# A three-layer transformer step in fp32: convolution jobs fed by the centered residual with both norms' rows applied behind PSUM, and a ring of nine weight slots for the experts

## The reference, cut to what matters

```python
# end of layer b
h = layer_norm(ALPHA * h + gate * y, ln_g[1], ln_b[1])        # eps 1e-5
# start of layer c
h1 = rms_norm(h, g_norm1) * (1.0 + sc1) + sh1                  # eps 1e-6
u = h1 @ w_in                                                  # 1024 x 2560
q, k, v, ga, gb = split(u, 5 parts of 512)
x = ga * sigmoid(gb)
y = causal_depthwise_conv(x, width 31) + conv_b                # then layer norm, silu
mix = concat(attention(q, k, v), y) @ w_out                    # added to h, gated
...
# experts: 4 groups of 8, top 2 of one group for each token
out += w * ((silu(x @ w_gate[e]) * (x @ w_up[e])) @ w_down[e]) # 32 experts, 3 x 2 MB each
```

## Time and profile before

| | |
|---|---|
| median of 3 runs | 1282.6 us (1281.47 to 1284.01) |
| the profiled execution | 1282.18 us, span 1280.4 us |
| PE busy | 1219.5 us, 95% |
| VectorE busy | 432.8 us, 34% |
| ScalarE busy | 297.4 us, 23% |
| mean granted TensorE clock | 0.975 of 2.4 GHz |
| read from HBM | 309.40 MB, mean 243 GB/s |

### The profile page before, as it was taken

The page is one execution under the profiler, slowest core; times in us unless marked ns, Lnnn a source line. Parts: engine busy times, 40 slices in busy tenths (PEclk is TensorE's granted clock), DMA queues, the critical chain, the costliest instruction groups (busy, mean ns, idle before and its releaser), DMA issues.

```text
span 1280.4 us, 14605 instructions
## 1 busy us (share of the span) xinstructions
PE 1219.5 (95%) x5832; PEld 660.7 (52%) x5832; DVE 432.8 (34%) x1076; ACT 297.4 (23%) x683; POOL 23.0 (2%) x33
## 2 busy tenths in 40 slices
PE   4999999989999999999899889999999999999997
PEld 2446446654474446667688457544444444444442
DVE  1211008972341000492419853222222223222223
ACT  0000017870240001371220242211111111111102
POOL 0000000000001000120000000000000000000000
PEclk9899999999989999999999889999999999999999
DMA  9921515003253321556615744869999999999994
GB/s 345 389 103 66 197 67 196 2 18 142 106 196 91 112 86 66 156 143 220 235 66 178 282 195 165 353 273 399 426 429 428 429 429 427 428 429 428 428 425 170
DMA packets 82028, 311.28 MB, mean 243 GB/s; under 512 B 18097, under 2 KB 18940, under 8 KB 69178
## 3 DMA queue, kind: packets, MB, share of 16 engines
q1 hardware_dynamic: 78384, 309.56, 61.7%
q10 hardware_dynamic: 3386, 0.86, 0.3%
q0 software_dynamic: 208, 0.17, 0.1%
HBM read 309.40 MB, written 1.18 MB: 243 GB/s over the span
## 4 chain that ended last, share of the span: by engine, by line
PE 70%; DMA 17%; DVE 9%; ACT 1%; issue 1%; SPq 1%; DVEq 0%; ACTq 0%
PE ps L643 19%; DMA ring<-in_w_exp_up 15%; PE ps L967 13%; PE ps L751 9%; PE ps L639 5%; PE ps L999 4%; DVE G L1634 4%; PE ps L584 3%; PE ps L701 3%; PE ps L715 3%; PE ps L688 3%; PE ps L933 2%; PE ps L945 2%; PE ps L802 2%; PE ps L595 2%; DMA ring<-in_w_ada 2%
## 5 line engine op out<-in xcount | busy, mean ns | idle before, releaser
L643 PE MATMUL ps<-U,ring 128*128 128x512 f32 (+1 forms) x800 | 267.2, 495 | 5.0 <-ACT U L1190 3.6
L967 PE MATMUL ps<-ring,prob 128*64 128x512 f32 x976 | 217.6, 593 | 5.9 <-DMA ring<-in_w_exp_up 4.7
L643 PEld LDWEIGHTS ps<-U,ring 128*128 128x128 f32 x800 | 153.3, 192 | 112.3 <-issue 99.9
L967 PEld LDWEIGHTS ps<-ring,prob 128*64 128x64 f32 x976 | 71.1, 137 | 144.4 <-issue 131.2
L999 PE MATMUL ps<-ring,prob 128*64 128x512 f32 x512 | 113.4, 595 | 0.0
L751 PE MATMUL ps<-U,ring 128*128 128x256 f32 (+1 forms) x384 | 111.6, 451 | 0.0
L751 PEld LDWEIGHTS ps<-U,ring 128*128 128x128 f32 x384 | 72.5, 190 | 37.3 <-issue 31.0
L1796 DVE TENSOR_TENSOR prob<-ps,prob 128x512 f32<-128x512 f32 x16 | 17.2, 1078 | 200.4 <-PE ps L967 200.4
L639 PE MATMUL ps<-ring,U 128*128 128x512 f32 (+1 forms) x224 | 83.1, 531 | 0.0
L999 PEld LDWEIGHTS ps<-ring,prob 128*64 128x64 f32 x512 | 35.3, 137 | 66.6 <-issue 66.6
L1091 ACT ACTIVATE prob<-ps,soft 128x512 f32<-128x512 f32 (+2 forms) x112 | 64.3, 593 | 12.5 <-DVE soft L1398 10.5
(11 more groups left out here) (252 smaller groups left out, 1050.9 us busy)
## 6 DMA issues: line engine op xcount, KB each, us to landing
ring<-in_w_exp_gate SPq DMA_DIRECT2D x30, 2048.0 KB, 15.1
ring<-in_w_exp_down SPq DMA_DIRECT2D x30, 2048.0 KB, 12.2
ring<-in_w_exp_up SPq DMA_DIRECT2D x29, 2048.0 KB, 17.3
ring<-in_w_ada SPq DMA_DIRECT2D x12, 2048.0 KB, 15.0
ring<-in_w_mod SPq DMA_DIRECT2D x12, 2048.0 KB, 8.1
ring<-in_b_w_in SPq DMA_DIRECT2D x8, 2048.0 KB, 8.6
ring<-in_a_w_in SPq DMA_DIRECT2D x5, 2048.0 KB, 19.8
ring<-in_w_in SPq DMA_DIRECT2D x5, 2048.0 KB, 8.4
```

Source lines behind the costliest of these rows:

```text
L643: last = mm(ps[:, b, 0:wid], w[:, col:col + P], src[:, k, 0:wid], start=(k == 0), stop=(k == KT - 1))
L967: last = mm(ps[x * CAP:(x + 1) * CAP, 2 + i, :], xg[:, k, x * CAP:(x + 1) * CAP], chunk(n, 2 * i + x)[0][:, k, :], start=(k == 0), stop=(k ...
```

## The change

First part. The b and a jobs of `c_in` (8 of 18) no longer read the finished `h1T` but `raw` = centered H times the gains' product (ScalarE, `gg`), with two more columns that carry the shifts (`RAW` = 258). They can start as soon as H is centered. VectorE takes each job out of PSUM times the row 1/std (`take_half`), and later applies 1/rms (`times_rms`); ScalarE makes the sigmoids from that, and VectorE the product (`gate`). The two sums of eight matmuls become sums on VectorE and one or two matmuls (`hsum2`, `sqsum2`). The q, k, v jobs still read `h1T`. Chunk 5 of `mod_a` moves behind the eight jobs, and its column is taken during the convolution.

Second part. K, G and Q stay slots of the ring until the last pair: chunk 6n+c lies in slot (6n+c) mod 9. Nine slots and six chunks repeat after three pairs, so pairs 0 to 2 are written out and the loop runs over four rounds of three pairs.

```diff
-        jobs = [("b", m, 0, m * P, "act") for m in range(4)]
+        jobs = [("b", m, 0, m * P, "dve") for m in range(4)]
...
-        def chunk(n, c):
-            second, first = isinstance(n, int) and n == 1, isinstance(n, int) and n == 0
-            if second and c < SLOTS // 2:
-                return (K, G, Q)[c][:, :].rearrange("p (k n) -> p k n", k=KT), extra_in, 16 * SLOTS // 2
-            s = c if first else (c + SLOTS // 2) % SLOTS
-            count = ROUNDS + 1 if first else ROUNDS + n + (s < SLOTS // 2)
-            return (dslot if c >= 4 else slot)(s), full[s], count * 16
+        WIDE = SLOTS + 3
+        BY = 3
+        def chunk(n, c, turn=0):
+            if isinstance(n, int) and n < PAIRS:
+                s, use = (6 * n + c) % WIDE, (6 * n + c) // WIDE + 1
+            elif isinstance(n, int):
+                s, use = c, 6 * PAIRS // WIDE + 1 + n - LATE
+            else:
+                q, j = turn
+                s, use = (c, 6 * PAIRS // WIDE + 1 - LATE + n) if q is None else (
+                    (6 * j + c) % WIDE, q * 2 + ((6 * j + c) // WIDE + 1))
+            home = ring[:, s, :] if s < SLOTS else (K, G, Q)[s - SLOTS][:, :]
+            count = use + ROUNDS if s < SLOTS else use
+            return home.rearrange("p (k n) -> p k n", k=4 if c >= 4 else KT), full[s], count * 16
...
+            def freed(n, c):
+                sp.wait_ge((up_done, down_done, down_done, gate_done, gate_done, up_done)[c], n - 1 if c < 3 else n)
...
-            with sp.Fori(3, LATE) as pair:
-                stream(pair, pair)
+            load_pair(2, 4, lambda c: freed(2, c))
+            with sp.Fori(1, LATE // BY) as q:
+                for j in range(BY):
+                    n = q * BY + j
+                    load_pair(n, q * (2 * BY) + 2 * j, lambda c: freed(n, c), (q, j))
...
-            norm_stats("lnb", sq, S, tk["b_out", "dve"], ("mod_a", 2, 1))
-            feature_sum(4, meanm, sq2, KT, S, nm["rms1", "sq"], nm["rms1", "var"])
-            in_proj("c_in", h1T, {"a": S, "b": S, "q": S, "k": S})
+            def raw_c(i):
+                ...
+                pe.wait_ge(*((tk["b_out", "dve"], 5 + i) if i < 4 else (tk["c_in", "dve"], i - 3)))
+                for k in range(KT):
+                    if i == 0:
+                        pe.wait_ge(raw_ok, KT + k + 1)
+                    last = mm(ps[:, i % 4, 0:RAW], slot(n)[:, k, (i % 4) * P:(i % 4 + 1) * P], raw[:, k, :],
+                              start=(k == 0), stop=(k == KT - 1))
+                last.then_inc(st["c_in"], 1)
...
+            stream("mod_a", 4, 6)
+            for i in range(3):
+                raw_c(i)
+                if i == 1:
+                    square_sum("lnb", 5, 3 + KT - 1)
+            for i in range(3, 2 * 4):
+                raw_c(i)
+                if i == 4:
+                    square_sum("rms1", 4, 3 + 2 * KT - 2)
+            fold("mod_a", 4, 2, 1, 7)
+            stream("mod_a", 5, 6)
+            fold("mod_a", 5, 2, 1, 7)
+            in_proj("c_in", h1T, {"q": S, "k": S}, skip=KT)
...
-                with pe.Fori(1 if r else 2, PAIRS - 1) as pair:
-                    experts(r, pair)
+                    experts(r, 2)
+                    with pe.Fori(1, LATE // BY) as q:
+                        for j in range(BY):
+                            experts(r, q * BY + j, turn=(q, j))
...
+            take_half(0)
+            for j in range(KT):
+                dve.wait_ge(nm["lnb", "sq"], KT)
+                v.scalar_tensor_tensor(H[:, j, 0:S], H[:, j, 0:S], vc("ln_g", 8 + j), lnrow[:, 0:S], ALU.mult, ALU.mult
+                                       ).then_inc(scaled, 1)
+            take_half(1)
+            take_half(2)
...
+            for m in range(4):
+                times_rms(m).then_inc(half_ok, 1)
+            for j in range(KT):
+                v.tensor_tensor(h1T[:, j, :], H[:, j, 0:S], rmsrow, ALU.mult).then_inc(scaled, 1)
+            dve.wait_ge(zero_ok, 1)
+            step(times_rms(4))
+            for m in range(1, 4):
+                take_half(4 + m)
+                settle()
+                gate(m - 1)
+                step(times_rms(4 + m))
+            settle()
+            gate(3)
```

More of the change, by code:

```diff
@@ L946, in scatter, with experts @@
                        start=True, stop=True).then_inc(scat, 1)
-            def experts(r, pair, first=False, final=False):
+            def experts(r, pair, first=False, final=False, turn=0):
                 n = r * PAIRS + pair
@@ L1614, in _ @@
-            take_mod2(CHUNKS["mod_a"] + 6, 16, 16, 24, 7)
-            dve.wait_ge(nm["lnb", "out"], KT)
-            invert("rms1", S)
-            scale_all(h1T, H, S)
-            dve.wait_ge(zero_ok, 1)
-            for m in range(4):
-                dve.wait_ge(st["c_in"], 4 + m + 1)
-                dve.wait_ge(tk["c_in", "act"], 4)
-                v.tensor_tensor(glu[:, m, CONV_W - 1:], ps[:, m, 0:S], sigb[:, m, :], ALU.mult
-                                ).then_inc(tk["c_in", "dve"], 1)
@@ new lines, in _, with add_squares @@
+            residual("b_out", 1, ((0, S),), add_up_b)
+            dve.wait_ge(nm["lnb", "mean"], 1)
+            for j in range(KT):
+                v.tensor_tensor(H[:, j, 0:S], H[:, j, 0:S], ps[:, 4, 0:S], ALU.subtract).then_inc(nm["lnb", "cent"], 1)
+            def add_squares(N, j, base):
+                dve.wait_ge(nm[N, "sq"], j + 1)
+                if j >= 2:
+                    dve.wait_ge(sqsum_ok, base + j - 1)
+                v.tensor_tensor(sqsum2, sq2[:, 0, :] if j == 1 else sqsum2, sq2[:, j, :], ALU.add).then_inc(sqsum_ok, 1)
@@ new lines, in _, with half_of, take_half, times_rms @@
+            for j in range(1, KT):
+                add_squares("lnb", j, 3)
+            dve.wait_ge(nm["lnb", "std"], 1)
+            step(v.reciprocal(lnrow[:, 0:S], lnrow[:, 0:S]))
+            settle()
+            def half_of(i):
+                return (half_a if i >= 4 else half_b)[:, i % 4, :]
+            def take_half(i):
+                dve.wait_ge(st["c_in"], i + 1)
+                v.tensor_tensor(half_of(i), ps[:, i % 4, 0:RAW], lnrow, ALU.mult).then_inc(tk["c_in", "dve"], 1)
+            def times_rms(i):
+                dve.wait_ge(tk["c_in", "dve"], i + 1)
+                t = half_of(i)
+                return v.scalar_tensor_tensor(t[:, 0:S], t[:, 0:S], t[:, S:S + 1], rmsrow, ALU.add, ALU.mult)
@@ new lines, in gate @@
+            def gate(m):
+                dve.wait_ge(sig_ok, m + 1)
+                t = half_a[:, m, :]
+                step(v.scalar_tensor_tensor(glu[:, m, CONV_W - 1:], t[:, 0:S], t[:, S + 1:S + 2], sigb[:, m, :],
+                                            ALU.add, ALU.mult))
+            take_half(0)
+            for j in range(KT):
+                dve.wait_ge(nm["lnb", "sq"], KT)
+                v.scalar_tensor_tensor(H[:, j, 0:S], H[:, j, 0:S], vc("ln_g", 8 + j), lnrow[:, 0:S], ALU.mult, ALU.mult
+                                       ).then_inc(scaled, 1)
```

136 lines of the change are left out of this document (81 added, 55 removed).

## The result

The changed kernel takes **1251.0 us** (median of 4 runs, 1245.4 to 1253.1) where the kernel before takes 1282.7: a ratio of 0.976, 95% interval 0.974 to 0.978. The forecast was 1255.4. The profiled execution took 1253.05 us, with a span of 1251.3. That is what to set against the 1282.2 and the span of 1280.4 that the prediction worked from: the difference of the spans is 29.1 us, 26.8 were forecast.

The account below looks back on a forecast made before the run. Besides PE, busy 95%, it saw two bounds: the convolution's late start on VectorE ahead of attention, and the experts' weight stream. 1282.2 - 20.1 - 6.7 = 1255.4 us; forecast range 1252.5 to 1258.5 (0.60), 80% range 1250 to 1264.

Parts of the forecast that it names:

- The forecast's case: Whole kernel: both parts gain as summed, time 1252.5 to 1258.5 us; chance 0.60.
- case E: Whole kernel: more is gained, through the clock in attention, time under 1252.5 us; chance 0.07.
- the clock in attention: Start of attention: PE idles less, so the granted clock may give 0 to 3 us more; left out of the sum.
- Mean and first job: Start of the c_in jobs: PE's work between last residual and job 0 shrinks from 23.4 to 2.9 us.
- Jobs: The eight c_in jobs on PE: 3.48 us each, 28.7 us with the sums between them.
- Second norm: Beside the c_in jobs: ScalarE's 16 shift and square instructions take 6.7 us; at 8 us PE waits 1.
- rival B: Seam to attention: the thin cover tears, PE reaches q 3 to 6 us late, 1258.5 to 1261.5 us; chance 0.11.
- VectorE behind the last job: Before the convolution: VectorE's work after the last c_in job grows from 0.5 to 1.8 us.
- The seam's term: From last residual to attention: the convolution starts 20.1 us earlier, with 0.2 us for `take_mod2` added inside it.
- PE is late next: Under the convolution: PE is ready within 0.3 us of need; each us lost ahead of q comes back whole.
- The ring: Experts' weights: nine slots remove all waits for up chunks, 6.7 us gained, with a margin of 8 us.
- Rivals A and D: PE's expert loop: A, returns stall, 1262 us, chance 0.15; D, body refetched every round, slower, 1300 us, chance 0.03.

Follow-up runs that it names:

- after_more: The changed kernel itself, unaltered, run again in a later group: 1251.2 us, ratio 0.979 to the kernel before.
- ring8: Changed kernel with eight weight slots instead of nine, PE's loop holding four expert pairs and passed three times: 1254.6 us, ratio 0.978 to the kernel before.
- body6: Changed kernel with nine slots kept, PE's loop holding six expert pairs instead of three and passed twice: 1255.5 us, ratio 0.981 to the kernel before.

## Why the prediction was right, point by point

The forecast's case was right in its mechanisms, and the profiled execution lies inside it (1253.05). The median is 4.4 us under the forecast and so in case E, which had 0.07. Some of the nearness is luck: two terms are missing from the sum, the clock in attention (some 3.3 us gained) and the jump at the end (2.3 us lost), and they nearly cancel.

- **Mean and first job.** 2.9 us from the last residual to job 0 were forecast, 617.36 - 614.34 = 3.0 are measured. PE has no gap from there to the end of the jobs.
- **Jobs.** Eight jobs with the two sums: 28.7 forecast, 29.1 measured (617.4 to 646.5). A job takes 3.49 us (10.48 / 3), 3.48 were taken.
- **Second norm.** ScalarE's 16 instructions in turn were taken at 6.7 us and took 5.8 (628.2 to 634.0). Nothing waited for them, since job 4 ran until 635.3. The cover of rival B did not tear.
- **VectorE behind the last job.** 1.8 forecast, 1.8 measured (646.5 to 648.29). The convolution starts 33.95 us after the last residual, where it was 53.5.
- **The seam's term** of 20.1 less the 0.2 for `take_mod2` was 19.9. Against the first profile of before it is 19.5, against the other two with the old seam 18.4 to 18.5, because those had less of the lower clock in the jobs of `c_in`.
- **PE is late next.** q was forecast at 36.0 us after the residual, it starts at 36.4; the streams' end at 84.3, measured 84.9. The second scores find VectorE just busy: no wait. The experiments on both sides (2.5 of 3.5 us lost, 3.6 of 22.2 gained) show that the cover is thin. It is 0.9 us where 0.3 was stated, so the prediction's sentence that each us of PE comes back whole holds only behind the first 0.9.
- **The clock in attention** was left out, with 0 to 3 us as its bounds. It should have stood in the sum. From attention to pair 0 it is 89.4 to 91.2 us in the three profiles with the old seam, and 86.0 to 88.2 in the nine with the new seam, the whole convolution and no work added on PE. The means are 90.5 and 87.2: 3.3 us. The total time at the lower clock does not tell them apart: this stretch has 27.3 us of it in the first profile of before and 30.7 in `after_more`, which is still 1.1 us shorter. What counts is where it lies. In the three old profiles it has set in before the 24 folding records, which then take 5.28 us; in the nine new ones they take 2.84 to 4.11 (3.99 in the first profile). From attention's start to the end of those folds it is 10.2 to 10.6 us with the old seam and 7.4 to 8.6 with the new one, 2.5 us less in the mean. So 2.5 of the 3.3 us are gained in the part that holds these folds. No experiment held the clock fixed, so this cause is argued and not shown, and the other 0.8 us are open.
- **The ring.** 6.7 forecast, 6.7 to 6.8 measured, with either seam. For the margin of 8 us the trace has 6.1: the last up chunk of pair 15 landed at 1212.6, its matmuls began at 1218.7. It shrinks by 0.8 us for each pair, as forecast (0.75). From pair 14 on eight slots leave less than 2 us.
- **Rivals A and D.** No packet came on PE's queue at the returns, no pair is late. The Trainium skill, "Runtime: NRT & Kernel Launch", section "Instruction fetch mechanics", has a taken branch fetch when its target is outside a window of two pages. For PE the trace disagrees: bodies of 3.4 and 4.5 packets run without a fetch. The Trainium skill also gives PE room for 2048 instructions in that section; as a limit for loops that isn't borne out either, since 1,700 were fetched anew.
- **The step that failed** is the sum's silence about the end of the program. It counts VectorE's added instructions by their time alone. They also move all code behind them against the packets in which it is loaded, and the jump at the end now lands in one that is fetched first: 2.3 us lost. The rule on taken branches in the same section of the Trainium skill, which I weighed for PE's loop alone, agrees with what VectorE shows here: 2.9 us with a packet on q14 in the gap, 0.6 without one.

By means of profiles the terms come to 18.8 (seam, 101.6 to 82.8) + 3.3 + 6.7 - 2.3 = 26.5 us. The medians of all runs shown (36 of before, 14 of after) differ by 1281.4 - 1251.4 = 30.0. Some 3.5 us of it are not placed. They may lie in the clock of runs that were not profiled, and that stays open.

## What to carry to other kernels

When a change adds or removes instructions on an engine, look at every taken branch behind them, not only at loops: its price hangs on where its target lies in the packets of instructions, and a few idle instructions can move it back. Where two engines' ends lie within 3 us of each other, say how far each can be shortened before the other holds: halving the convolution would have been worth 3.6 us, not 22. And compare stretches between two landmarks of the trace rather than totals, when the same code ahead of the edit scatters by more than the term in question.

## What was not expected of the hardware

- In these traces PE runs a loop body of 4.5 packets of 16 KB (about 1,140 instructions) without a fetch (`ring8`); at 6.7 packets (about 1,700, `body6`) ten packets come in the second pass, and PE idles 2.3 us at the return. What lies between the two wasn't run.
- VectorE's branch takes 2.8 to 3.1 us to the next instruction when a packet is fetched in between, against 0.6 us. 50 or 60 instructions more make the difference; 128 more, or 6 fewer, make none. The packets of q14 are 8 KB, which is 128 instructions if one takes 64 bytes, as on PE (16 KB for about 256). The queue is not VectorE's alone.
- Stretches at the lower granted clock in code that didn't change shift the seam between 611.2 and 619.6 us, more than the change's second part is worth.
